# Two transformer blocks on one core: second keys and queries of block two as 512-column records, with more adding DMAs

## The reference, cut to what matters

```python
n = rmsnorm(h, norm_mix_g)
c_a, c_g, q, k, v, qi, ki, wi, gc, ga = split(n @ w_in)
y_conv = conformer_conv(c_a, c_g)              # 31 taps per channel, layernorm, silu, @ w_conv_out
y_attn = dsa_attention(q, k, v, qi, ki, wi)    # index scores, top 64 keys, 8 heads
h = h + (g_conv * y_conv + g_attn * (y_attn @ w_attn_out)) @ w_mix_out
h = h + cross_attention(rmsnorm(h, norm_x_g), rmsnorm(mem, norm_mem_g))
h = h + square(relu(rmsnorm(h, norm_ffn_g) @ w_ff1)) @ w_ff2
return rmsnorm(h, norm_final_g)
```

## Time and profile before

| | us |
|---|---|
| median of three runs | 903.67 (903.33 to 904.20) |
| the profiled execution | 904.27 |
| its span | 902.1 |
| TensorE products busy | 895.1 (99%) |
| VectorE busy | 696.8 (77%) |
| ScalarE busy | 554.1 (61%) |
| POOL busy | 41.4 (5%) |

### The profile page before, as it was taken

The page is one execution under the profiler, slowest core; times in us unless marked ns, Lnnn a source line. Parts: engine busy times, 40 slices in busy tenths (PEclk is TensorE's granted clock), DMA queues, the critical chain, the costliest instruction groups (busy, mean ns, idle before and its releaser), DMA issues.

```text
span 902.1 us, 13580 instructions
## 1 busy us (share of the span) xinstructions
PE 895.1 (99%) x4940; PEld 768.9 (85%) x4940; DVE 696.8 (77%) x1353; ACT 554.1 (61%) x952; POOL 41.4 (5%) x52
## 2 busy tenths in 40 slices
PE   9999999999999999999999999999999999999997
PEld 7988877788888888888889998888889988888886
DVE  6788899667766666667998999999976786666666
ACT  7767878745644444456566657776745755744544
POOL 0410000000000000000010100100000000000000
PEclk9999999999999999999999999999999999999999
DMA  9977677665465555556797898487564377555551
GB/s 340 322 212 199 179 198 223 250 204 182 141 230 196 192 189 191 190 193 213 215 258 216 235 248 240 123 228 233 175 215 164 113 209 239 187 186 187 187 187 47
DMA packets 96930, 183.48 MB, mean 203 GB/s; under 512 B 8096, under 2 KB 18144, under 8 KB 96608
## 3 DMA queue, kind: packets, MB, share of 16 engines
q1 hardware_dynamic: 92128, 166.35, 56.3%
q0 software_dynamic: 4368, 15.73, 9.4%
q10 hardware_dynamic: 368, 0.52, 0.2%
HBM read 164.69 MB, written 1.05 MB: 184 GB/s over the span
## 4 chain that ended last, share of the span: by engine, by line
PE 97%; DVE 2%; issue 0%; ACT 0%; DVEq 0%; ACTq 0%
PE pb L511 95%; PE pb L515 1%; PE pb L725 1%; DVE wlo L1766 0%; DVE CC L2053 0%; DVE UU L2085 0%; DVE SM L1909 0%; DVE ST L2002 0%; DVE ST L2009 0%; DVE PC L2019 0%; DVE PC L2004 0%; DVE PC L1997 0%; DVE PC L2007 0%; DVE CC L2050 0%; DVE X L2531 0%
## 5 line engine op out<-in xcount | busy, mean ns | idle before, releaser
L1162 ACT ACTIVATE whi<-raw 128x1024 fp32r<-128x1024 f32 (+2 forms) x304 | 309.2, 1038 | 127.9 <-PE pb L511 118.7
L1766 DVE TENSOR_TENSOR wlo<-raw,whi 128x1024 fp32r<-128x1024 f32 (+1 forms) x269 | 318.4, 1212 | 85.1 <-ACT whi L1162 84.6
L511 PE MATMUL pb<-XT,whi 128*128 128x512 f32 (+1 forms) x1232 | 283.9, 358 | 0.3 <-DVE CC L2085 0.3
L511 PE MATMUL pb<-whi,ZO 128*128 128x512 f32 (+1 forms) x776 | 239.5, 388 | 0.0
L511 PEld LDWEIGHTS pb<-XT,whi 128*128 128x128 f32 x1232 | 200.8, 189 | 24.3 <-issue 1.9
L511 PEld LDWEIGHTS pb<-whi,ZO 128*128 128x128 f32 x776 | 145.2, 188 | 29.4
L511 PE MATMUL pb<-XT,wlo 128*128 128x256 f32 (+1 forms) x1032 | 166.4, 282 | 0.0
L511 PEld LDWEIGHTS pb<-XT,wlo 128*128 128x128 f32 (+1 forms) x1032 | 153.2, 190 | 14.0
L511 PE MATMUL pb<-whi,XT 128*128 128x512 f32 (+1 forms) x544 | 163.6, 391 | 0.0
L511 PE MATMUL pb<-wlo,ZO 128*128 128x512 f32 (+1 forms) x388 | 148.8, 387 | 0.0
L511 PEld LDWEIGHTS pb<-whi,XT 128*128 128x128 f32 x544 | 101.4, 189 | 21.2 <-issue 0.7
(11 more groups left out here) (253 smaller groups left out, 653.2 us busy)
## 6 DMA issues: line engine op xcount, KB each, us to landing
raw<-in_w_in SPq DMA_DIRECT2D x105, 512.0 KB, 4.9
raw<-in_w_ff SPq DMA_DIRECT2D x64, 512.0 KB, 5.4
raw<-in_w_up SPq DMA_DIRECT2D x32, 512.0 KB, 4.7
raw<-in_w_down SPq DMA_DIRECT2D x32, 512.0 KB, 4.7
wlo<-raw POOLq DMA_DIRECT2D x29, 512.0 KB, 6.2
raw<-in_w_branch_b SPq DMA_DIRECT2D x8, 512.0 KB, 5.6
raw<-in_w_out SPq DMA_DIRECT2D x8, 512.0 KB, 4.0
raw<-in_wx_kv SPq DMA_DIRECT2D x8, 512.0 KB, 5.5
```

The lines of the kernel that those rows point to most:

```text
L511: return e.matmul(o, l, r, start=start, stop=stop, skip_group_check=True)
L1162: return e.activation(o, i, ACT.Copy, scale=scale)
L1766: e.tensor_tensor(wlo[u % NW][:, 0:c], raw_tile(u)[:, 0:c], whi[u % NW][:, 0:c].bitcast(F32), ALU.subtract).then_inc(lo, 1)
```

## The change

k1, q0 and q1 join `LATE`, so they go as k0 does, and leave `by_act`. In the last unit of k0, k1, q0 and q1 VectorE makes its four adds before the side steps of that unit. From unit 186 every even unit of `by_dma`'s stretch is summed by DMA, in place of every third (24 units there in place of 20: 188, 190, 194, 196, 200, 202, 206, 208 are new, 189, 195, 201, 207 go). `TAPS2` has fewer taps in the steps of k1 to q1 (steps 28 to 36) and more later; the sum is the same 248. The second piece of the first convolution moves one step. At the end the earlier chunks and X, multiplied by the inverse of the row factor, are put into bank 0 ahead of the last products, which sum onto them; ScalarE squares the tile from the bank, VectorE multiplies it by the gain.

```diff
-TAPS2 = (..., 3, 1, 1, 5, 5, 4, 7, 4, 5, 7, 6, 4, 8, 5, 6, 7, 5, 4, 8, 4, 1, 7, 5, 4, 5, 4, 3, 7, 0, 4, 7, 4, 9)
+TAPS2 = (..., 2, 1, 1, 3, 2, 3, 5, 3, 2, 7, 6, 4, 8, 8, 4, 8, 5, 5, 8, 7, 0, 8, 6, 5, 6, 7, 2, 8, 1, 5, 7, 7, 5)
-LATE = ('b2_qi', 'b2_k0')
+LATE = ('b2_qi', 'b2_k0', 'b2_k1', 'b2_q0', 'b2_q1')
+        FGAIN = st(1)
-        by_dma += [u for u in range(first["b2_qi"] + 1, first["b2_wa1"]) if u % 3 == 0 and u != first["b2_ki"]]
+        by_dma += [u for u in range(first["b2_qi"] + 1, first["b2_wa1"]) if (u % 3 == 0 and u != first["b2_ki"] if u < 186 else u % 2 == 0)]
-        by_act = {..., "b2_cg1", "b2_ki", "b2_k1", "b2_q0", "b2_q1", "b2_v0", "b2_v1"}
+        by_act = {..., "b2_cg1", "b2_ki", "b2_v0", "b2_v1"}
@@ down_end, TensorE
-                            mm(o, ZT[:, a:a + P], h[:, k, c0:c1], c0 > 0 and kt == 0, False)
+                            mm(o, ZT[:, a:a + P], h[:, k, c0:c1], False, False)
@@ end, ScalarE
+            e.wait_ge(end_tile, 5)
+            e.activation(MSQ[:, 768:1024], PB[0][:, 256:512], ACT.Square, scale=NR[N_FFN][1],
+                         accum_out=NLAST).then_inc(end_sq, 1)
@@ run, VectorE
-            def run(name, *sides, begin=0):
+            def run(name, *sides, begin=0, wait_last=False):
-                    for s in sides:
+                    for s in sides if q < count[name] - 1 or not wait_last else ():
@@ taps2: the second and third of the sums of finished tiles move from step 37 to 39 and from 48 to 50
-            taps = [taps1(0, (1, 3, 5, 8)), taps1(1, (2, 3, 5, 6))]
+            taps = [taps1(0, (1, 4, 5, 8)), taps1(1, (2, 3, 5, 6))]
             for name in ("b2_k0", "b2_k1", "b2_q0", "b2_q1"):
-                run(name, side, taps)
+                run(name, side, taps, wait_last=True)
                 for f in range(4) if name in LATE else ():
                     add_right(name, f, (KT2 if name[3] == "k" else QT2)[:, 4 * int(name[4]) + f, :])
+                for s in (side, taps):
+                    next(s, None)
@@ end, VectorE
-            e.scalar_tensor_tensor(out=X[:, D + 768:2 * D], in0=PB[7][:, 256:512], scalar=NR[N_FFN][1],
-                                   in1=X[:, D + 768:2 * D], op0=ALU.mult, op1=ALU.add).then_inc(end_upper, 1)
+            e.scalar_tensor_tensor(out=PB[0][:, 256:512], in0=X[:, D + 768:2 * D], scalar=NMEAN[N_FFN][1],
+                                   in1=PB[7][:, 256:512], op0=ALU.mult, op1=ALU.add).then_inc(end_upper, 1)
+            step(e.tensor_scalar(FGAIN, NR[N_FFN][1], float(D) ** 0.5, None, ALU.mult))
+            after_step()
...
-            e.wait_ge(end_upper, 1)
-            end_add(5, 1, 768, 1024, 0)
-            e.wait_ge(end_x, 5)
-            e.wait_ge(end_sq, 4)
-            e.scalar_tensor_tensor(out=MSQ[:, 768:1024], in0=X[:, D + 768:2 * D], scalar=1.0, in1=X[:, D + 768:2 * D],
-                                   op0=ALU.mult, op1=ALU.mult, accum_out=NLAST).then_inc(end_sq, 1)
             end_sum_others(1)
-            end_gain(5, 1, 768, 1024).then_inc(end_g, 1)
+            e.wait_ge(end_sq, 5)
+            e.scalar_tensor_tensor(out=XS[:, D + 768:2 * D], in0=PB[0][:, 256:512], scalar=FGAIN, in1=GF[:, 768:1024],
+                                   op0=ALU.mult, op1=ALU.mult).then_inc(end_g, 1)
             end_factor(1)
+            e.wait_ge(end_g, 2)
```

More of the change, by code:

```diff
@@ L45 @@
 GAIN = {T_X: "norm1", T_MEM: "normmem", T_2: "norm2", T_MIX: "normmix", T_XA: "normx", T_FFN: "normffn"}
-TAPS2 = (4, 4, 2, 4, 4, 4, 6, 0, 7, 3, 6, 3, 3, 7, 4, 5, 3, 5, 0, 8, 0, 1, 3, 1, 0, 0, 1, 1, 3, 1, 1, 5, 5, 4, 7, 4, 5, 7, 6, 4, 8, 5, 6, 7, 5, 4, 8, 4, 1, 7, 5, 4, 5, 4, 3, 7, 0, 4, 7, 4, 9)
+TAPS2 = (4, 4, 2, 4, 4, 4, 6, 0, 7, 3, 6, 3, 3, 7, 4, 5, 3, 5, 0, 8, 0, 1, 3, 1, 0, 0, 1, 1, 2, 1, 1, 3, 2, 3, 5, 3, 2, 7, 6, 4, 8, 8, 4, 8, 5, 5, 8, 7, 0, 8, 6, 5, 6, 7, 2, 8, 1, 5, 7, 7, 5)
 EAGER = ("b2_qi", "b2_ki", "mv", "b2_cg1", "b2_k0", "b2_k1", "b2_q0", "b2_q1", "b2_v0", "b2_v1")
-LATE = ('b2_qi', 'b2_k0')
+LATE = ('b2_qi', 'b2_k0', 'b2_k1', 'b2_q0', 'b2_q1')
 HALVES = ("b1_c0", "b1_x0", "b1_c1", "b1_x1", "b1_b0", "b1_b1", "mk")
@@ L306, in build @@
         out_a, out_d = sem("tile_out_act"), sem("tile_out_dve")
-        by_act = {"b1_q", "b1_kv", "b1_w", "b1_gb0", "b1_gb1", "b1_ga0", "b1_ga1", "mv", "b2_cg1", "b2_ki", "b2_k1", "b2_q0", "b2_q1", "b2_v0", "b2_v1"}
+        by_act = {"b1_q", "b1_kv", "b1_w", "b1_gb0", "b1_gb1", "b1_ga0", "b1_ga1", "mv", "b2_cg1", "b2_ki", "b2_v0", "b2_v1"}
         tile_at, out_at, bank_of, bank_free = {}, {}, {}, {}
@@ L2233, in taps2 @@
                                     sum_tiles((0, 1), y_made, 2)
-                                if at == 37:
+                                if at == 39:
                                     sum_tiles((2, 3), y_made, 4)
-                                if at == 48:
+                                if at == 50:
                                     sum_tiles((4, 5), y_made, 6)
```

## The result

The changed kernel takes 906.72 us (median of 8 executions, 904.72 to 908.02), the kernel before 904.13 beside it (8 executions, 903.33 to 905.01): ratio 1.0026, 95% interval 1.0017 to 1.0034. It is slower. The profiled execution took 906.74 us, with a span of 904.5. VectorE was busy 695.7 us, ScalarE 558.2, POOL 44.9.

The account below looks back on a forecast made before the run. TensorE, 97% of the span, was taken to bound the kernel. Terms -1.08 - 0.05 - 0.50 + 2.34 + 0.35 + 0.20 = +1.26 us put the median at 904.9, range 901.6 to 906.6.

Parts of the forecast that it names:

- the forecast's own mechanism: Whole kernel: the summed terms, with waits at q0 and q1, give median 904.9, range 904.2 to 905.8; chance 0.40.
- no change: Whole-kernel class: measured time between 901.86 and 905.48, not told from the kernel before; chance 0.45.
- longer records: k1, q0, q1: one 512-column product per weight tile in place of two saves 0.36 us a group, 1.08 in all.
- wait at q0: Start of q0: TensorE waits for VectorE's late k1 adds to free the bank, 0.72 + 0.07 us.
- wait at q1: Start of q1: TensorE waits for VectorE's late q0 adds, 1.48 + 0.07 us.
- score pass and last head: Attention: VectorE's late score pass costs 0.35 us, ScalarE's late scaling of the last head 0.20.
- first tap: First convolution, block one: moving a tap removes the wait for c1's add; gain 0.05 us, bounds 0 and 0.54.
- end: After the last product: early add and squaring from the bank bring the reciprocal 0.5 us sooner, bounds 0.3 and 0.6.
- adding DMAs: Units 188 to 208: more sums by DMA cost 0 on the path, covered by units made four ahead.
- Rival A: k1 to q1: VectorE's adds come in time, waits vanish; 902.0, or 901.5 with the tap's gain; chance 0.30.
- rival C: k1, q0, q1: the longer record saves nothing, groups stay at 11.52 us; 906.0; chance 0.04.
- Rival B: Value stage and heads: VectorE's 2.5 us lag stays, three or four heads wait 0.4 to 0.6 each; 906.5; chance 0.22.

Follow-up runs that it names:

- e6: Changed kernel with adds first only in k1 and q0, unit 179 summed by DMA for 180, two taps moved off unit 175's step: 903.37 us.
- e4: Kernel before with only the new end and the moved first-convolution tap: 903.43 us, ratio 0.9993.
- e2: Kernel before with only the new list of units summed by DMA: 904.84 us, ratio 1.0011.
- e7: Changed kernel with k1, q0, q1 in short records and the old order of adds; new list, taps, end kept: 904.30 us, ratio 1.0008.
- e8: As e6, but from unit 200 on only 201, 204 and 207 summed by DMA: 902.87 us, ratio 0.9989.
- e10: As e8, with three more 512 KB adding DMAs between unused tiles, holding no raw slot: 905.41 us, ratio 1.0012.
- e1: Changed kernel with the old list of units summed by DMA, every third: 908.27 us, ratio 1.0043.
- e3: Changed kernel with units 206 and 208 taken out of the DMA-summed list: 906.33 us, ratio 1.0028.
- e5: Changed kernel with adds ahead of the last side steps only in k1 and q0: 904.95 us, ratio 1.0008.

## Where the prediction was right, and where it was wrong

The forecast was 904.9, +1.23 on its median of before; measured is +2.59. By the ratio that is 906.0 on the median of 903.67 that the forecast was made from, inside its range of 901.6 to 906.6; the median itself lies 0.1 above that. It moved the way that was forecast. But it lies outside 904.2 to 905.8, the range of the forecast's own mechanism: the wide range holds it because it was drawn to reach into rivals A and B, and it was neither of them. That much is luck. The likeliest class, no change, had 0.45; slower came, which had 0.35. Step by step, in the profiled executions:

| step | forecast | measured |
|---|---|---|
| longer records | -1.08 | -1.07 (e6: 45.73 to 44.66) |
| wait at q0 | 0.79 | 0.76 (due 492.77 + 22.32 = 515.09, start 515.85) |
| wait at q1 | 1.55 | 1.58 (528.52 - 515.85 - 11.16, and 0.07 up to v0) |
| score pass and last head | 0.55 | 0.37 (v0 to DG) |
| first tap | -0.05 | 0.0 (e4) |
| end | -0.50 | -0.58 |
| adding DMAs | 0 | +1.82 (1.15 from DG to LNS, 0.67 from LNS to GC) |

The measured rows add up to +2.88, and the profiled executions lie 2.47 apart, mostly because the changed kernel's came to k0 0.55 us earlier. That is within the spread of the traces: the eleven kernels with the moved tap start k0 at 492.62 to 493.87, on average at 493.34, and the one before at 493.32.

**The records and the waits** came out as the running account of VectorE's queue had them: k0 to v0 grew by 1.25, and -1.08 + 2.34 = 1.26 was forecast. Rival A fell with the waits, rival C with groups of 11.16. The Trainium skill (TensorE: Matmul & The Clock Gate, "Wait — 56ns, not 53.3ns?") adds about 2.5 ns to each warm product; by that, as an estimate, 96 products fewer would have saved 0.24. This trace disagrees: 1.07 over 96 products, 11 ns each.

**The failed step** is "0 on the path" for the adding DMAs; it measured 1.82 us. It took their median landing of 6.2 us as a fixed cost, where the slowest of those 29 sums took 9.8, and it allowed ScalarE up to 1 us for the slots. It didn't ask how busy the DMA engines were in the stretch that gets the new sums. The windows view would have warned it: 0.78 before, and two sums more in 26 us bring 0.98. There loads and sums stretch each other (12.7 and 9.8 us), and ScalarE stood 3.22 us. The second half of the step is the cover. The four units ahead did cover the weights: TensorE waits for no unit there. But they cover nothing else, and the layernorm's steps, behind those units in the queues of ScalarE and VectorE, passed 1.82 us of the wait on. The runs agree: e2 and e7 have the late loads without the longer records (e7 the loss too), e8 has the longer records without late loads, e10 brings them back.

**Rival B** was priced at 906.5, near the result, but its place was not where the time went: the heads lost 0.37. e1 shows that its lag would have been there had the list stayed as it was: 3.0 us more, though mostly at the last head and the diagonal, not in three or four heads at 0.4 to 0.6. The four subtractions fewer that the prediction set against it are what e1 takes away.

What stays open: why one load takes 12 to 13 us in the changed kernel, e6 and e7, but at most 8.7 in e2 and 8.0 in e3, and what chooses the executions in which it does. The traces narrow it. Of their 544 loads from 500 to 640 us, the 104 with no sum in flight beside them took at most 8.0 us, the 310 with one at most 10.2, the 130 with two or more up to 13.2. And each of the six over 12 us landed within 0.4 us of a sum that was issued after it; in the changed kernel unit 210's load at 625.93, the sum of 208, issued 4.6 us after that load, at 625.73. No run changed the order of DMAs within a queue.

## What to carry to other kernels

Price a DMA that is moved or added by the stretch where it will fly (how busy the DMA engines are there, what flies beside it, the longest landing), not by its median landing over the whole run. A cover of some units ahead protects those units; ask also what other work stands behind them in the same queue. A high share is a warning and no verdict: from 539 to 560 us the kernel before has 0.96, with nine raw slots, and no engine waits for a load. When work moves from a full engine to DMAs, look for the stretch in which the transfers have least room, and leave that part where it was: in e8, with the new list up to unit 198 only and VectorE's adds in time, the change gains 1.3 us in place of losing 2.6. An extra operation on a full engine can be priced by carrying that engine's queue on row by row; here that gave the stage from k0 to v0 to within 0.1 us in four kernels (the changed one, e5, e6, e7).

## What was not expected of the hardware

From 600 to 626 us a 512 KB load that flew 3.9 to 6.2 us in e8 took up to 12.7 beside the sums of the changed kernel and 13.2 in e10, and a sum 9.8 and 11.1 in place of 5.6. The kernel before shows the beginning of it: one load of 8.6 us there, beside a sum of 9.0. The same program can then give executions up to 3.3 us apart (the changed kernel, share 0.98), while those of e8, at 0.82, lie within 1.2. The spread goes with the share only roughly: e3 has the widest, 3.5, and in its profiled execution the share is 0.85.
